# Fourteen projection tiles as seven pairs of seven block products, with block sums and root multiplies on GpSimd

## What is computed

```python
h = rmsnorm(x, g_mix)                      # x: 544 x 1024
z = h @ w_in                               # queries and keys here as 16 tiles of 128 features
q, k = rope(rmsnorm(z_head, g_head), pos)  # 15 of the 16 tiles, heads of 64 features
mk = rmsnorm(rmsnorm(mem, g_mem) @ w_mk, g_mk)   # 4 tiles of 128 features x 256 memory tokens
```

## Time and profile before

| | us |
|---|---|
| three runs, median | 1272.08 |
| lowest and highest | 1269.83, 1274.61 |
| profiled execution, span from first to last instruction | 1270.2 |
| PE busy | 1242.2 |
| DVE busy | 668.9 |
| ACT busy | 363.6 |
| POOL busy | 204.0 |

### The profile page before, as it was taken

How to read it: one execution, slowest core, us unless ns; L and a number is a source line. 1 busy time by engine, 2 the same in 40 slices (tenths; PEclk the granted TensorE clock), 3 DMA queues, 4 the chain that set the end, 5 groups by cost and what they waited for, 6 DMA issues and landing times.

```text
span 1270.2 us, 19608 instructions
## 1 busy us (share of the span) xinstructions
PE 1242.2 (98%) x6934; PEld 979.2 (77%) x6934; DVE 668.9 (53%) x1517; ACT 363.6 (29%) x743; POOL 204.0 (16%) x396
## 2 busy tenths in 40 slices
PE   7999999999999999999999999999999999999999
PEld 6788765887877766766788887687888888888887
DVE  3776612585555525124135643339878788873331
ACT  4766741444444422112100015321121212110000
POOL 1000000433334425124000110131000101000000
PEclk9999999899999999999999999999999999999999
DMA  6342314423322689899292311022222222312240
GB/s 227 122 163 67 141 47 178 154 71 98 101 68 86 225 289 353 311 325 333 68 402 96 133 61 40 26 74 70 80 84 83 84 83 83 121 54 92 92 157 18
DMA packets 80868, 170.17 MB, mean 134 GB/s; under 512 B 10529, under 2 KB 48354, under 8 KB 79874
## 3 DMA queue, kind: packets, MB, share of 16 engines
q1 hardware_dynamic: 62962, 110.94, 26.1%
q10 hardware_dynamic: 13648, 47.49, 10.0%
q0 software_dynamic: 4160, 10.49, 2.5%
HBM read 159.07 MB, written 9.81 MB: 133 GB/s over the span
## 4 chain that ended last, share of the span: by engine, by line
PE 91%; DVE 4%; ACT 2%; issue 2%; DMA 1%; POOL 0%; ACTq 0%; DVEq 0%; SPq 0%; POOLq 0%
PE ps L2544 19%; PE ps L2581 11%; PE ps L2323 10%; PE ps L1617 9%; PE ps L491 9%; PE ps L1085 6%; PE ps L2356 4%; PE ps L546 3%; PE ps L1018 2%; PE ps L990 2%; PE ps L1004 2%; PE ps L473 1%; PE ps L2404 1%; PE ps L494 1%; PE ps L531 1%
## 5 line engine op out<-in xcount | busy, mean ns | idle before, releaser
L2544 PE MATMUL ps<-arena 128*128 128x272 f32 x1120 | 257.1, 392 | 0.8 <-DVE arena L2883 0.8
L2544 PEld LDWEIGHTS ps<-arena 128*128 128x128 f32 x1120 | 212.7, 190 | 45.1 <-DVE arena L2883 1.2
L491 PE MATMUL ps<-arena 128*128 128x272 f32 x512 | 122.9, 399 | 6.7 <-DVE arena L606 6.7
L1617 PE MATMUL ps<-arena 128*128 128x272 f32 x512 | 121.8, 395 | 0.5 <-PE ps L1717 0.5
L2581 PE MATMUL ps<-arena 128*128 128x272 f32 x528 | 121.8, 392 | 0.0
L491 PEld LDWEIGHTS ps<-arena 128*128 128x128 f32 x512 | 98.9, 194 | 27.4 <-issue 6.7
L1617 PEld LDWEIGHTS ps<-arena 128*128 128x128 f32 x512 | 95.8, 190 | 26.9 <-issue 8.4
L2581 PEld LDWEIGHTS ps<-arena 128*128 128x128 f32 x528 | 100.3, 190 | 20.7
L1085 PEld LDWEIGHTS ps<-arena 128*128 128x128 f32 x768 | 90.3, 196 | 11.9 <-issue 11.4
L1085 PE MATMUL ps<-arena 128*128 128x128 f32 (+1 forms) x768 | 95.9, 283 | 1.8 <-DVE arena L1212 1.8
L2271 ACT ACTIVATE arena<-arena 128x560 f32<-128x560 f32 x44 | 35.3, 848 | 159.2 <-DVE arena L2898 152.5
(11 more groups left out here) (374 smaller groups left out, 1736.7 us busy)
## 6 DMA issues: line engine op xcount, KB each, us to landing
arena<-in_w_close SPq DMA_DIRECT2D x68, 512.0 KB, 3.5
arena<-in_pages_cmp SPq DMA_DIRECT2D x128, 128.0 KB, 2.2
arena<-in_past_va ACTq DMA_DIRECT2D x6, 2048.0 KB, 11.9
arena<-in_w_down SPq DMA_DIRECT2D x16, 704.0 KB, 6.0
arena<-in_past_ka ACTq DMA_DIRECT2D x6, 1792.0 KB, 11.1
arena<-in_w_close ACTq DMA_DIRECT2D x16, 512.0 KB, 6.3
arena<-in_w_proj SPq DMA_DIRECT2D x15, 512.0 KB, 3.4
arena<-in_pages_ks SPq DMA_DIRECT2D x96, 64.0 KB, 4.2
```

Source lines behind the costliest of these rows:

```text
L491: last = pe.matmul(ps[:, 2 * (j % 2) + a, 0:HALF], w, h[:, k, a * HALF:(a + 1) * HALF], start=(k == 0), stop=(k == KD - 1))
L1617: last_one = pe.matmul(ps[:, gate_bank(q), 0:HALF], ring[:, n % CLOSE_RING, k * P:(k + 1) * P], m.h[:, k, half * HALF:(half + 1) * HALF], ...
L2544: last = pe.matmul(ps[:, bank(f, i), 0:HALF], w[:, k * P:(k + 1) * P], halved[:, rhs, k, :], start=(k == 0), stop=(k == 3))
```

## The change

Tiles 2 to 15 are taken as seven pairs (a, b) = (2 + 2p, 3 + 2p). The weights of a pair are a 2 x 2 matrix of blocks W11, W12 (tile a, k 0 to 3 and 4 to 7), W21, W22 (tile b), and h is B11, B12 (k 0 to 3, first and second half of the tokens), B21, B22 (k 4 to 7). In place of eight block products of four matmuls the pair takes seven, in Winograd's form of Strassen's scheme: W11 B11, W12 B21, S1 T1, S2 T2, S3 T3, S4 B22, W22 T4. POOL computes T1 to T4 once (`turn`) and S1 to S4 for each pair (`half_sums`). The parts are called x1 (first), y, x2, z1, x3, z2, x4, by the bank that they go to; x parts of a pair go on top of each other in bank p % 2, z parts in bank 3, y in bank 2, and ACT copies the state of a bank out between two parts (`keep`), for which the next part on that bank waits. DVE puts the quarters of the pair together ("11", "22", "12"); the fourth is x4 itself. The first part of the next pair goes before x4.

The roots of a pair are taken together: two Ln, then two Exp, in `logs` and `guesses`. The gains of the heads go into rope (`scalar_tensor_tensor` in place of `tensor_tensor`), and the multiply of the tile by its root moves from DVE to POOL (`rooted_tile`). `columns` follows pair 0. `hm` is scaled in pairs 2 to 5. In the next stage the 2 MB load of `w1` moves behind the last product, since its place holds T1 to T4 now; `tiles_ready` waits for POOL as well. `refined` waits for the root before where both use `bend`.

The core of the diff:

```diff
+    half_sum = at(8704, 4, 4 * P)
+    one_1, one_2, one_3, one_4 = at(10752, 2, HALF), at(11296, HALF), at(11568, HALF), at(11840, HALF)
+    means = (at(39304, NT), m.packed[:, 3 * MTOK:3 * MTOK + NT])
+    roots = (at(39848, NT), m.packed[:, 3 * MTOK + NT:3 * MTOK + 2 * NT])
+    turned = at(25208, 4, 4, HALF)
+    b11, b12, b21, b22 = h[:, 0:4, 0:HALF], h[:, 0:4, HALF:NT], h[:, 4:8, 0:HALF], h[:, 4:8, HALF:NT]
...
+    WORK = [("tile", 0), ("tile", 1)] + [("pair", p) for p in range(NPAIR)]
...
+    ROOTS = {("tile", 1): ("x",), ("pair", 0): (1, "mem"), ("tile", NTILE): in_pair(NPAIR - 1)}
+    ROOTS |= {("pair", p): in_pair(p - 1) for p in range(1, NPAIR)}
...
+            before = j - RING
+            if before in (0, 1):
+                sp.wait_ge(z_full, full("tile", before))
+            elif before >= 2:
+                p, second = divmod(before - 2, 2)
+                sp.wait_ge(z_full, full("x4" if second else "y", p))
+                sp.wait_ge(pool_made, pooled("s", p, S4))
...
+        def turn(to, a, b, after=None):
+            if after is not None:
+                pool.wait_ge(pool_made, pooled("t", after))
+            pool.tensor_tensor(turned[:, to], a, b, ALU.subtract).then_inc(pool_made, 1)
+
+        def half_sums(p):
+            a, b = in_pair(p)
+            w11, w12 = (ring[:, a % RING, 4 * i:4 * i + 4, :].rearrange("p k n -> p (k n)") for i in range(2))
+            w21, w22 = (ring[:, b % RING, 4 * i:4 * i + 4, :].rearrange("p k n -> p (k n)") for i in range(2))
+            for j in (a, b):
+                pool.wait_ge(chunk_in[j % RING], 16 * (j // RING + 1))
+            if p >= 1:
+                pool.wait_ge(z_full, full("z1", p - 1))
+            pool.tensor_tensor(half_sum[:, S1], w21, w22, ALU.add).then_inc(pool_made, 1)
+            pool.wait_ge(pool_made, pooled("s", p, S1))
+            pool.tensor_tensor(half_sum[:, S2], half_sum[:, S1], w11, ALU.subtract).then_inc(pool_made, 1)
+            if p >= 1:
+                pool.wait_ge(z_full, full("x3", p - 1))
+            pool.tensor_tensor(half_sum[:, S3], w11, w21, ALU.subtract).then_inc(pool_made, 1)
+            if p >= 1:
+                pool.wait_ge(z_full, full("z2", p - 1))
+            pool.wait_ge(pool_made, pooled("s", p, S2))
+            pool.tensor_tensor(half_sum[:, S4], w12, half_sum[:, S2], ALU.subtract).then_inc(pool_made, 1)
+
+        def rooted_tile(r):
+            pool.wait_ge(summed, made("root", r))
+            pool.wait_ge(roped, r)
+            z = m.z[:, order[r], :]
+            pool.tensor_tensor(z, z, roots[r % 2], ALU.mult).then_inc(pool_made, 1)
...
+        pool.wait_ge(h_ready, KD)
+        pool.wait_ge(squared, KD)
+        turn(T1, b12, b11)
+        turn(T2, b22, turned[:, T1], T1)
+        turn(T3, b22, b12)
+        turn(T4, b21, turned[:, T2], T2)
...
+        half_sums(0)
+        for p in range(NPAIR):
+            if p >= 1:
+                for r in ROOTS["pair", p - 1]:
+                    if r != "mem":
+                        rooted_tile(r)
+            if p + 1 < NPAIR:
+                half_sums(p + 1)
+        for r in late_roots:
+            rooted_tile(r)
...
+                if r not in ("x", "mem") and 3 <= r <= NTILE:
+                    act.wait_ge(pool_made, pooled("tile", r - 2))
...
+        def keep(kind, p, bank, to):
+            act.wait_ge(z_full, full(kind, p))
+            act.copy(to, ps[:, bank, 0:HALF]).then_inc(squared, 1)
+
+        def keep_first(p):
+            if p >= 2:
+                act.wait_ge(summed, made("11", p - 2))
+            keep("x1", p, p % 2, one_1[:, p % 2])
+
+        def pair(p):
+            a, b = in_pair(p)
+            rs = ROOTS["pair", p]
+            if p >= 1:
+                act.wait_ge(summed, made("12", p - 1))
+            keep("x2", p, p % 2, one_2)
+            keep("z1", p, Z_BANK, one_4)
+            logs(rs)
+            keep("x3", p, p % 2, one_3)
+            guesses(rs)
+            if p + 1 < NPAIR:
+                keep_first(p + 1)
+            act.wait_ge(summed, made("12", p))
+            if p >= 1:
+                act.wait_ge(sum_full, nth(a - 2))
+            act.activation(square[:, 0, :], raw[:, 0, :], ACT.Square).then_inc(z_out, 1)
+            act.wait_ge(roped, b - 2)
+            keep("x4", p, p % 2, raw[:, 1, 0:HALF])
+            act.wait_ge(sum_full, nth(b - 2))
+            act.wait_ge(squared, kept("x4", p))
+            act.activation(square[:, 1, :], raw[:, 1, :], ACT.Square).then_inc(z_out, 1)
...
+            if j == NTILE:
+                pe.wait_ge(squared, kept("x4", NPAIR - 1))
+                pe.wait_ge(h_ready, 2 * KD)
+            elif j == NTILE + 1:
+                pe.wait_ge(summed, made("11", NPAIR - 1))
...
+                for i, r in enumerate(ROOTS.get(("tile", j), ())):
+                    if k == (2, KD - 2)[i] if j == NTILE else k == KD - 2:
...
+        def first_part(p):
+            a, _ = in_pair(p)
+            pe.wait_ge(chunk_in[a % RING], 16 * (a // RING + 1))
+            if p < 2:
+                pe.wait_ge(z_out, 1)
+            else:
+                pe.wait_ge(squared, kept("x4", p - 2))
+            part(p % 2, of_ring(a, 0), b11, True)
+
+        def pair(p):
+            a, b = in_pair(p)
+            rs = ROOTS["pair", p]
+            if p == 0:
+                pe.wait_ge(z_out, 2)
+            else:
+                pe.wait_ge(summed, made("11", p - 1))
+            part(Y_BANK, of_ring(a, 4), b21, True)
+            sums(rs[0])
+            pe.wait_ge(pool_made, pooled("s", p, S2))
+            pe.wait_ge(squared, kept("x1", p))
+            part(p % 2, of_sum(S2), turned[:, T2], False)
+            if p >= 1:
+                pe.wait_ge(summed, made("12", p - 1))
+            part(Z_BANK, of_sum(S1), turned[:, T1], True)
+            sums(rs[1])
+            pe.wait_ge(pool_made, pooled("s", p, S3))
+            pe.wait_ge(squared, kept("x2", p))
+            part(p % 2, of_sum(S3), turned[:, T3], False)
+            pe.wait_ge(pool_made, pooled("s", p, S4))
+            pe.wait_ge(squared, kept("z1", p))
+            part(Z_BANK, of_sum(S4), b22, False)
+            if p + 1 < NPAIR:
+                first_part(p + 1)
+            pe.wait_ge(chunk_in[b % RING], 16 * (b // RING + 1))
+            pe.wait_ge(squared, kept("x3", p))
+            part(p % 2, of_ring(b, 4), turned[:, T4], False)
...
+            row = raw[:, j % 2, :]
+            if j == 1:
+                dve.wait_ge(z_out, 2)
+            else:
+                p, second = divmod(j - 2, 2)
+                if second:
+                    dve.wait_ge(squared, kept("x4", p))
+                dve.wait_ge(summed, made("22" if second else "12", p))
+            step.done(dve.stream_shuffle(shuffled[:, :], row, SWAP))
+            step.done(dve.scalar_tensor_tensor(out=m.z[:, t, :], in0=row, scalar=g_heads[:, 0, t:t + 1], in1=cos[:, :],
+                                               op0=ALU.mult, op1=ALU.mult))
             step.wait(step.n - 1)
-            step.done(dve.tensor_tensor(shuffled[:, :], shuffled[:, :], sin[:, :], ALU.mult))
+            step.done(dve.scalar_tensor_tensor(out=shuffled[:, :], in0=shuffled[:, :], scalar=g_heads[:, 1, t:t + 1],
+                                               in1=sin[:, :], op0=ALU.mult, op1=ALU.mult))
...
+            a, b = in_pair(p)
+            if p >= 1:
+                for r in ROOTS["pair", p - 1]:
+                    if r == "mem":
+                        refined(r, mem_root[:, :])
+                        step.wait()
+                    else:
+                        refined(r, roots[r % 2], summed)
+            rope(b - 2)
+            mean_of(ROOTS["pair", p][0])
+            dve.wait_ge(z_full, full("y", p))
+            dve.wait_ge(squared, kept("x1", p))
+            if p >= 1:
+                dve.wait_ge(z_out, a - 1)
+            put("11", p, raw[:, 0, 0:HALF], ps[:, Y_BANK, 0:HALF], one_1[:, p % 2])
+            mean_of(ROOTS["pair", p][1])
+            if p == 1:
+                dve.wait_ge(col_full, 1)
+                step.done(dve.tensor_copy(column[:, :], ps[:, 6, 0:QT + 1]))
+                step.wait()
+                dve.tensor_scalar(minus[:, :], column[:, :], -1.0, None, ALU.mult).then_inc(col_ready, 1)
+            if 2 <= p < 6:
+                for k in (2 * (p - 2), 2 * (p - 2) + 1):
+                    dve.scalar_tensor_tensor(out=hm[:, k, 0:MTOK], in0=mem[:, k, :],
+                                             scalar=m.g_model[:, KD + k:KD + k + 1], in1=mem_root[:, :],
+                                             op0=ALU.mult, op1=ALU.mult).then_inc(h_ready, 1)
+            dve.wait_ge(squared, kept("x3", p))
+            dve.wait_ge(z_out, b - 1)
+            put("22", p, raw[:, 1, HALF:NT], one_3, one_4)
+            dve.wait_ge(z_full, full("z2", p))
+            put("12", p, raw[:, 0, HALF:NT], ps[:, Z_BANK, 0:HALF], one_2)
+            rope(a)
...
+            if w == ("tile", NTILE):
```

(7 more changed lines are left out.)

178 lines of the change are left out of this document (108 added, 70 removed).

## The result

The changed kernel takes 1297.94 us (median of four runs, 1293.68 to 1298.67), the kernel before 1270.95 in the same session: a ratio of 1.0198, 95% interval 1.0175 to 1.0221. Slower, as forecast, but by 27 us instead of 9, and outside the range of 1266 to 1292. The profiled execution took 1293.68 us, span 1292.0, so 1.7 us lie around the span; the other three took 3.6 to 5 us more, at a mean granted clock of 0.986 to 0.989 against 0.991.

A forecast was written before the change was run, and what follows sets the result against it. PE was taken as the bound, each pair waiting on DVE's mean at 16.1 us; with head and tail the second value unit came 9.0 us later: span 1270.2 + 9.0 = 1279.2, 1.9 below the median, time 1281.0, range 1266 to 1292.

The forecast's parts named there:

- PE idles once per pair ahead of the second root's sums: Pair loop, sign of being right: PE waits there until DVE's mean releases it, 1.4 us late.
- the multiplications hold bend: Pair loop: POOL's multiply by the first root delays DVE's second-root ops 1.1 us; its next multiply holds cos 0.65.
- The head: Start to columns' end: x's sums at 24.8, columns' end 50.95 against 45.13 before, one pair 1 part done ahead.
- The tail: From z2 of pair 6 to the second value unit: 26.0 us, start at 168.4 against 159.45.
- rival 4: PE's clock halves after idle gaps: head and tail +1, or each pair's gap 3.2 us, giving 1297; chance 0.08.
- no meeting: Pair loop, lower bound if POOL and DVE ops never meet: 14.67 us per pair.
- the length of the pair: Pair loop: 16.1 us per pair, 5 x 16.1 from z2 of pair 1 to z2 of pair 6.
- S1 waits for z1 and falls behind the last add (0): Pair loop: POOL's S1 starts after the last add of DVE's rope, so it costs DVE 0 us.
- my plain list for DVE: Pair loop: DVE's work from z2's end to the first root's mean, without holds by POOL, 9.7 us.
- PE's way from the sums to z2's end: Pair loop: second root's sums, x3 and z2 on PE close the loop in 4.58 us.
- the forecast pause of 1.4 us: Pair loop: PE asks at 10.1 us after z2, is let on at 11.5, so it idles 1.4 us.
- From there PE is the bound in both, and all moves by as much: Behind the second value unit's start: everything later shifts by the same 9.0 us.

The follow-up runs named there:

- Experiment 1: Changed kernel with POOL multiplying only 8 of 544 columns of tiles 1 to 15 by their root: 1271.89 us, one execution.
- experiment 4: Changed kernel with DVE making the first root's mean before the second tile's rope, also at tile 16: 1279.85 us, ratio 1.0052.
- experiment 2: Changed kernel with POOL forming only 8 of 512 columns of each of S1 to S4: 1286.64 us, one execution.
- experiment 3: Changed kernel with S1 also waiting for the mean of the pair's first root: 1289.32 us, ratio 1.0131.
- experiment 6: Changed kernel, head reordered: ACT takes tile 1 before x's root, POOL makes pair 0's S1 to S4 before the memory sums: 1296.86 us, ratio 1.0198.
- experiment 12: Changed kernel with 112 already fulfilled wait instructions added to PE's stream: 1291.53 us, ratio 1.0151.
- experiment 10: Changed kernel with mean before second rope, reordered head, spread hm products, and four idle-bank matmuls before tile 16: 1272.65 us, ratio 1.0010.
- experiment 11: Changed kernel with mean before second rope, reordered head, spread hm products, and 112 fulfilled waits in PE's stream: 1270.27 us, ratio 0.9993.
- experiment 5: Changed kernel with PE multiplying into an idle bank during its pause before the second root's sums, from the third pair: 1290.27 us, ratio 1.0137.

## Why the prediction was right and wrong

**Right: direction, engine, place.** PE idles once per pair ahead of the second root's sums and DVE's mean releases it; the multiplications hold bend (forecast 1.1, measured 1.17) and cos (0.65 and 0.65). The head: last add of x's squares at 24.7, sums at 24.89 (24.8), columns' end 51.08 (50.95), z2 of pair 1 at 62.3 (61.95). The tail: 179.11 is 26.0 us behind z2 of pair 6, at 153.13; forecast 26.0. Both landmarks agree although PE ran at half clock behind its pauses of 3.85 and 4.50 us there, which the sum leaves out: 12 instructions took 5.6 us instead of 2.75 in the head, and the tail lost 1.8. As rival 4 said, most of that vanished in other waits: DVE's mean, for which the memory's sums wait, ended at 41.8, and PE came to them at 42.2; and unit 0 was copied only at 179.06, where PE now waited 0.2 us instead of the 1.9 of the sum. Experiment 1 is the bound "no meeting": 14.86 against 14.67.

The rule of the Trainium skill (SBUF — State Buffer, "SBUF: two separate sides") holds in the traces here: bend takes 1.90 us beside POOL's multiply and 0.72 without it, and in experiment 4 sin and add (1.78 and 1.68) go in turn with S1 and S2 (1.75 and 1.63). Its condition, two SBUF inputs on DVE, holds too: the mean beside S3 took 0.71 in experiment 4.

**Wrong: the length of the pair.** z2 of pair 1 to z2 of pair 6 took 90.8 us, not 80.5. The step that failed is "S1 waits for z1 and falls behind the last add (0)". The last add starts 0.04 us behind S1 and is held 1.07 us, in four of five pairs (4.3 us; the last pair makes no S1, and its pause is 1.73). Experiments 2 and 3 show it twice: without the sums, or with S1 a few us later, a pair is 16.6. By an estimate from the forecast's own terms (11.5 less 0.73 for the mean, 0.65 for the add and 0.2 for handovers) the add was to start 9.9 us behind z2 and S1 10.1; measured were 10.28 and 10.24. What turned the order round was small: my plain list for DVE was 9.7 us, the measured one 9.97 (12.86 less the three holds), and a quarter of a microsecond decided on a whole one. The remaining excess is that list (5 x 0.27 = 1.4) and PE's way from the sums to z2's end, 4.84 instead of 4.58 (1.3).

**Wrong: the clock, by its weight.** Rival 4 had 0.08 and a price of 3.2 us per pair. In the profiled execution two of five pairs fell to half clock, at 1.7 us each, 3.4 us. This excess hangs on the first: 13 pauses of 1.7 to 1.8 us stand in the loops of the traces (all of experiments 2 and 3, and the last pair of the changed kernel and of experiments 6 and 12), and none was followed by half clock, against 7 of the 12 of 2.80 us. So at the forecast pause of 1.4 us the clock would most likely have stayed up, and I had not tied the two together: a longer pause costs twice. Together 4.3 + 1.4 + 1.3 + 3.4 = 10.4, where 10.3 us were to be explained.

**Not seen: the stop behind.** "From there PE is the bound in both, and all moves by as much" was off by 2.1 us. Taking instructions out of PE's stream moved all later code to other places in it, and one stop of 1.0 to 2.1 us came up, with half clock behind it in some kernels. Experiments 10, 11 and 12 show that the place in the stream decides whether and behind which instruction it comes; its length does not hang on that alone, for the same stream of PE has 1.03 us in experiment 1, 1.58 in the changed kernel and 2.04 in experiment 2. Why it vanished with 46 and 112 instructions more, instead of moving further forward, stays open. That it is a late refill of the instruction stream is an inference. The Trainium skill (Runtime: NRT & Kernel Launch, "Instruction fetch mechanics") says that instructions are fetched in blocks and calls the cost of crossing from one to the next mostly hidden; no run here shows the fetching itself, and this stop would be the exception, behind some 150 instructions that follow each other in 0.03 us while the DMA engines are full.

In sum: forecast span 1279.2, measured 1292.0; 10.3 of the 12.8 us lie in the loop, 0.4 in the head, 2.1 in the stop. The median lies 5.9 us above the profiled span, where I had allowed for 1.8: 1.7 around the span, and 4.3 by which the other executions, at a lower mean clock (0.986 to 0.989), were longer than the profiled one. That makes 12.8 + 4.1 of the 16.9 us by which 1281.0 was missed.

**Where the expected gain went.** A pair saves 1.83 us of PE, 12.8 in all. In the changed kernel the loop costs more than that by waits on DVE; without them (1: 1271.9, one execution) head and tail eat it. The traces show PE waiting there, 3.85, 2.73 and shorter times; I read that as follows: x's root, the memory's root and the last two roots are chains through ACT and DVE that PE's products used to cover, and there are fewer of these. With mean first, another head and spread hm products (11) the loop is PE's own and head and tail lose least: 1270.27, not to be told from the kernel before (ratio 0.9974 to 1.0012).

## What to carry to other kernels

Before a shorter product list pays, the chains that it covered must fit into the shorter time: count the loop through the other engines from the last product back to the first wait. Operations moved to GpSimd are not off VectorE's list where VectorE reads two SBUF operands; each costs it about 1.1 us here, unless it stands in a pause or beside an op with a PSUM operand, and where two such ops start within 0.3 us of each other, count both orders. Put what another engine waits for (the mean) ahead of what nobody waits for (the rope): a swap of two lines gave 18 of the 27 us back.

## What the runs showed of the hardware

- In one execution the same pause of 2.80 us ended at full clock twice and at half clock twice; in three traces at half clock 7 times of 12. Pauses of 3.84 to 4.52 us were followed by half clock each time, 15 times in nine traces; those of 1.7 to 1.8 us in the loop never, 13 times; but a pause of 1.87 us, ended at 233.94 in the kernel before, was the earlier trace rows. In experiment 5 pauses of 0.51 us kept the clock full. Each half-clock stretch in the loop cost 1.7 us.
- A stop of 1.0 (experiment 1) to 2.1 us (experiment 3) in the midst of products, with no wait in the code, depends on how many instructions stand ahead in PE's stream: 8 more moved it 8 instructions forward (experiment 10), 112 more, none of which does any work, took it away and with it the half clock behind (experiment 11).
- POOL takes 1.27 us for a 512-wide f32 tensor_tensor alone, 1.34 for 544, and up to 1.77 for 512 when it alternates with DVE (experiment 4), which then takes 1.7 to 1.9 instead of 0.72.
